# A two-block kernel on one core: new keys stage, expert stage with 4 KB rows and outputs put off by a block, output weights split early

## The reference, cut to what matters

```python
# merge and output of each mixer: mixed (512 x 1024) @ w_out (1024 x 1024), then x = layer_norm(ALPHA * x + ...)
# experts: 32, top 4 of them for each token, in blocks of up to 128 tokens of one expert
hb = xb @ w_exp_in[e] + b_exp_in[e]            # 128 x 1024 @ 1024 x 2048
g = jnp.minimum(hb[:, :D_FF], SWIGLU_LIMIT)
u = jnp.clip(hb[:, D_FF:], -SWIGLU_LIMIT, SWIGLU_LIMIT)
a = g * jax.nn.sigmoid(SWIGLU_ALPHA * g) * (u + 1.0)
y = a @ w_exp_out[e] + b_exp_out[e]            # 128 x 1024 @ 1024 x 1024
# compressed keys and values: 31 blocks of 32 positions, 16 apart, of each of 2 groups of width 64
blocks = src.reshape(B, S, G, dk)[:, blk_idx] + cmp_pos[None, None, :, None, :]
blocks = blocks.transpose(0, 3, 1, 2, 4).reshape(B, G, n_cmp, CMP_BLOCK * dk)
return jax.nn.gelu(blocks @ w1) @ w2           # w1: 2048 x 128, w2: 128 x 64
```

## Time and profile before

| | us |
|---|---|
| median of 3 runs (2675.25 to 2684.84) | 2681.73 |
| the profiled execution's own time | 2683.39 |
| its span | 2681.4 |
| PE busy | 2223.4 (83%) |
| DVE busy | 1728.8 (64%) |
| ACT busy | 1336.6 (50%) |
| POOL busy | 383.9 (14%) |
| expert stage, first to last product | 645.4 to 1880.6 |

### The profile page before, as it was taken

The page is one execution under the profiler, slowest core; times in us unless marked ns, Lnnn a source line. Parts: engine busy times, 40 slices in busy tenths (PEclk is TensorE's granted clock), DMA queues, the critical chain, the costliest instruction groups (busy, mean ns, idle before and its releaser), DMA issues. The chain is left out here.

```text
span 2681.4 us, 31345 instructions
## 1 busy us (share of the span) xinstructions
PE 2223.4 (83%) x10176; PEld 1775.4 (66%) x10176; DVE 1728.8 (64%) x2113; ACT 1336.6 (50%) x1452; POOL 383.9 (14%) x224
## 2 busy tenths in 40 slices
PE   4969879855999999999999999999158988885586
PEld 3747668654777777777777777777058666674564
DVE  4463511347899889989898989898620454457634
ACT  2333433225777777777777777776010343341130
POOL 0101134302111111111111111111000000000032
PEclk9989999966999999999999999999575677997888
DMA  5122033126999999999999999997470001010030
GB/s 185 32 102 55 16 95 94 63 67 244 343 350 365 351 349 354 361 350 347 357 362 349 347 357 362 349 348 274 162 141 16 9 0 47 24 47 0 19 107 32
DMA packets 305951, 524.83 MB, mean 196 GB/s; under 512 B 24055, under 2 KB 87551, under 8 KB 304525
## 3 DMA queue, kind: packets, MB, share of 16 engines
q1 hardware_dynamic: 287020, 486.59, 51.7%
q0 software_dynamic: 9504, 34.61, 3.3%
q10 hardware_dynamic: 9376, 2.98, 0.7%
HBM read 503.12 MB, written 26.78 MB: 198 GB/s over the span
## 5 line engine op out<-in xcount | busy, mean ns | idle before, releaser
L1370 DVE TENSOR_TENSOR piece_lower<-piece,moe_upper 128x2048 fp32r<-128x2048 f32 x384 | 870.2, 2287 | 120.7 <-ACT moe_upper L1302 120.7
L1302 ACT CAST moe_upper<-piece 128x2048 fp32r<-128x2048 f32 x384 | 727.5, 1911 | 112.2 <-PE bank L1242 103.9
L1240 PE MATMUL bank<-moe_upper,x_hi 128*128 128x512 f32 x1536 | 643.2, 419 | 0.0
L1242 PE MATMUL bank<-moe_upper,x_hi 128*128 128x512 f32 x1536 | 606.7, 395 | 0.0
L1241 PE MATMUL bank<-piece_lower,x_hi 128*128 128x512 f32 x1536 | 606.7, 395 | 0.0
L1242 PEld LDWEIGHTS bank<-moe_upper,x_hi 128*128 128x128 f32 x1536 | 289.8, 189 | 67.1
L1241 PEld LDWEIGHTS bank<-piece_lower,x_hi 128*128 128x128 f32 x1536 | 290.6, 189 | 62.1
L1240 PEld LDWEIGHTS bank<-moe_upper,x_hi 128*128 128x128 f32 x1536 | 291.6, 190 | 60.0
L1201 POOL COPY moe_dst<-row 128x1 uint32 x32 | 46.2, 1443 | 829.6 <-ACT moe_y L1289 829.6
L264 PE MATMUL bank<-const,xs 128*128 128x128 f32 x96 | 20.7, 386 | 96.7 <-DVE xs L235 96.7
L1293 ACT CAST x_hi<-bank 128x512 fp32r<-128x512 f32 x64 | 37.0, 578 | 108.9 <-PE bank L1248 108.9
(11 more groups left out here) (479 smaller groups left out, 4017.7 us busy)
## 6 DMA issues: line engine op xcount, KB each, us to landing
piece<-in_w_exp_in_dram SPq DMA_DIRECT2D x256, 1024.0 KB, 6.3
piece<-in_w_exp_out_dram SPq DMA_DIRECT2D x128, 1024.0 KB, 5.9
combine_ys<-y_slots SPq DMA_DIRECT2D x8, 1024.0 KB, 9.3
ahead<-in_w_in_dram SPq DMA_DIRECT2D x3, 2048.0 KB, 8.2
ahead<-in_w_in_dram SPq DMA_DIRECT2D x4, 1536.0 KB, 6.6
diff_raw<-in_w_in_dram SPq DMA_DIRECT2D x8, 512.0 KB, 5.1
band_raw<-in_w_in_dram SPq DMA_DIRECT2D x8, 512.0 KB, 5.1
ahead<-in_w_in_dram SPq DMA_DIRECT2D x8, 512.0 KB, 4.7
```

Of the source, the lines that this page charges most:

```text
L1240: nc.tensor.matmul(bank, hi[:, t, :], upper[u][:, t, :], start=False, stop=False)
L1242: done = nc.tensor.matmul(bank, lo[:, t, :], upper[u][:, t, :], start=False, stop=last and t == 3)
L1302: nc.scalar.copy(upper[h % SPLIT][:, :, :], ring[s][:, :, :]).then_inc(hi_ready, 1)
L1370: nc.vector.tensor_tensor(lower[s][:, :, :], ring[s][:, :, :], upper[h % SPLIT][:, :, :].bitcast(F32), ALU.subtract).then_inc(lo_ready, 1)
```

## The change

- **Experts.** A piece is now 128 partitions x 2 rows x 1024 columns (rows of 4 KB), 8 pieces into g and u, 4 into the output; one piece feeds two banks. The output product of block j-1 is put off into the iteration of block j, behind that block's input product: PE does 8 input pieces of block j, transposes the halves of block j-1's activations after pieces 3 and 4, waits for their lower parts, transposes the next tokens, then does the 4 output pieces of block j-1. The first iteration has 8 pieces, and a `last` part after the loop does the last output. Two iterations stand ahead of the loop, and one `If` guards a pair. The block count is rounded up to an even one, and every expert gets at least one block. `sg`, `g` and `u` are handled on DVE and ACT one iteration later.
- **Route.** SP issues the first 8 loads (expert 0) at once, behind the biases'. DVE has four more small operations and three more drains.
- **Output weights.** The first half of `w_out` is split in the stage before, on ACT and DVE (`output_upper`, `output_lower`); the second half's lower part moves from POOL to DVE, 3 tiles behind each row block.
- **Keys stage.** All loads move to SP at the stage's start. The two halves of a block's 32 positions now stand on the two halves of the partitions, so that a matmul sums over 128 rows and takes both groups' 62 columns: 16 matmuls for keys and 16 for values. ACT copies the projections to both halves of the partitions, shifted by 16.

The diff, cut to its core; where a part stands nested, eight spaces of indentation are left out:

```diff
+    for f in (NK - 2, NK - 1):
+        act.wait_ge(merged, f + 1)
+        gate(f, 0)
+        if f == NK - 1:
+            output_upper(nc, act, k)
+        gate(f, 1)
...
+    output_lower(nc, dve, k)
+    merge(NK - 1)
...
+def output_upper(nc, act, k):
+    act.wait_ge(k.ahead_in, k.ahead_loads)
+    for t in range(NK):
+        nc.scalar.copy(k.w_upper[:, t, :], k.ahead[:, t, :]).then_inc(k.output["w0_hi"], 1)
+def output_lower(nc, dve, k):
+    for t in range(NK):
+        dve.wait_ge(k.output["w0_hi"], NK * k.output.done["w0_in"] + t + 1)
+        split_lower(nc.vector, k.ahead[:, t, :], k.w_upper[:, t, :], k.ahead_lower[:, t, :])
...
-    for c in range(2):
-        act.wait_ge(*loaded[c])
-        for t in range(NK):
-            if c == 0:
-                nc.scalar.copy(m.hi[:, t, :], m_t[:, t, :]).then_inc(m_hi, 1)
-            nc.scalar.copy(w[c].hi[:, t, :], raws[c][:, t, :]).then_inc(w_hi, 1)
-@block.gpsimd
-def _(pool):
-    for c in range(2):
-        for t in range(NK):
-            pool.wait_ge(w_hi, 2 * NK * o + NK * c + t + 1)
-            split_lower(nc.gpsimd, raws[c][:, t, :], w[c].hi[:, t, :], w[c].lo[:, t, :]).then_inc(w_lo, 1)
+    for t in range(NK):
+        nc.scalar.copy(m.hi[:, t, :], m_t[:, t, :]).then_inc(m_hi, 1)
+    act.wait_ge(w1_in, 16 * o + 16)
+    for t in range(NK):
+        nc.scalar.copy(w[1].hi[:, t, :], raw1[:, t, :]).then_inc(w_hi, 1)
 @block.tensor
 def _(pe):
...
-                if i == 0:
-                    pe.wait_ge(w_lo, 2 * NK * o + NK * c + t + 1)
+                if n == NT:
+                    pe.wait_ge(w_lo, NK * o + t + 1)
...
+            for t in range(3 * n, min(3 * n + 3, NK)):
+                dve.wait_ge(w_hi, NK * o + t + 1)
+                split_lower(nc.vector, raw1[:, t, :], w[1].hi[:, t, :], w[1].lo[:, t, :]).then_inc(w_lo, 1)
...
-    col, kh = PIECES[h]
-    w = A["w_exp_in" if h < 8 else "w_exp_out"][0].rearrange("e (k p) n -> e p k n", p=P)
-    return w[ds(e, 1), :, 4 * kh:4 * kh + 4, col:col + 512].rearrange("o p k n -> (o p) k n")
+    col, pair = ((h // 4) * FF, h % 4) if h < INNER else (0, h - INNER)
+    w = A["w_exp_in" if h < INNER else "w_exp_out"][0].rearrange("e (k p) n -> e p k n", p=P)
+    return w[ds(e, 1), :, 2 * pair:2 * pair + 2, col:col + FF].rearrange("o p k n -> (o p) k n")
...
-    sp.wait_ge(expert_ready, 1)
-    e = sp.value_load(r.expert_i[0:1, 0:1], min_val=0, max_val=NE - 1)
-    for h in range(LOADED):
-        sp.dma_start(r.ring[h][:, :, :], weight_piece(A, e, h)).then_inc(r.piece_in[h], 16)
+    for h in range(INNER):
+        sp.dma_start(r.ring[h][:, :, :], weight_piece(A, 0, h)).then_inc(r.piece_in[h], 16)
...
-    nc.vector.tensor_scalar(nb[:, :], counts[:, :], 0.0, None, ALU.is_gt)
+    nc.vector.tensor_scalar(nb[:, :], counts[:, :], 0.0, None, ALU.is_ge)
...
+    nc.vector.tensor_scalar(r.expert[:, :], r.expert[:, :], float(NE - 1), None, ALU.min)
+    nc.vector.tensor_copy(total[:, 0:1], ends[:, NE - 1:NE])
+    dve.drain()
     nc.vector.tensor_copy(r.expert_i[:, 0:MAX_BLOCKS], r.expert[:, :])
-    nc.vector.tensor_copy(r.expert_i[:, MAX_BLOCKS:MAX_BLOCKS + 1], ends[:, NE - 1:NE])
-    dve.drain().then_inc(expert_ready, 1)
+    nc.vector.tensor_scalar(total[:, 1:2], total[:, 0:1], 1, None, ALU.bitwise_and)
+    dve.drain()
+    nc.vector.tensor_tensor(total[:, 0:1], total[:, 0:1], total[:, 1:2], ALU.add)
+    dve.drain()
+    nc.vector.tensor_scalar(r.expert_i[:, MAX_BLOCKS:MAX_BLOCKS + 1], total[:, 0:1], 2, None, ALU.subtract)
     for i in range(NT):
         nc.vector.tensor_tensor(dest[:, i, :], k.bank[i][:, 0:NE], starts[:, :], ALU.add)
...
+def each_pair(eng, iteration, last, before=None):
+    rest = eng.value_load(r.expert_i[0:1, MAX_BLOCKS:MAX_BLOCKS + 1], min_val=NE - 2, max_val=MAX_BLOCKS - 2)
     if before:
         before()
-    with eng.Fori(0, MAX_BLOCKS // 2) as q:
-        for p in range(2):
-            with eng.If(q * 2 + p < count):
-                body(q, p, q * 2 + p)
+    iteration(None, 0)
+    iteration(None, 1)
+    with eng.Fori(0, MAX_BLOCKS // 2 - 1) as q:
+        with eng.If(q * 2 < rest):
+            iteration(q, 0)
+            iteration(q, 1)
+    last(rest)
...
+    def iteration(q, p):
+        if is_first(q, p):
+            return
+        e = expert(at(q, p, 1))
+        for h in range(INNER):
+            load(e, slot(q, p, h), piece(q, p, h - LOADED), h)
+        e = expert(at(q, p, 1, -1))
+        for h in range(INNER, PIECES):
+            load(e, slot(q, p, h), piece(q, p, h - LOADED), h)
...
+        for t in range(2):
+            f = 2 * pair + t
+            for c in range(2):
+                to, cols = k.bank[bank + c][:, :], slice(512 * c, 512 * c + 512)
+                nc.tensor.matmul(to, hi[:, f, :], upper[u][:, t, cols], start=False, stop=False)
+                nc.tensor.matmul(to, hi[:, f, :], lower[s][:, t, cols], start=False, stop=False)
+                done = nc.tensor.matmul(to, lo[:, f, :], upper[u][:, t, cols], start=False, stop=f == NK - 1)
         done.then_inc(used, 1)
...
+    def iteration(q, p):
+        first = is_first(q, p)
+        pe.wait_ge(sel_ready, at(q, p, 1, 1))
+        pe.wait_ge(x_lo_ready, at(q, p, 2, 2))
+        for h in range(INNER):
+            if h % 4 == 0:
+                if not first:
+                    pe.wait_ge((g_ready, u_ready)[h // 4], at(q, p, 2))
+                for c in range(2):
+                    add_bias(p, h // 2 + c, FF * (h // 4) + 512 * c)
+            products(piece(q, p, h), slot(q, p, h), h, 2 * (h // 4), x_hi, x_lo)
+            if not first and h in (3, 4):
+                transpose_half(h - 3, at(q, p, 2, h - 4))
+        if not first:
+            pe.wait_ge(a_lo_ready, at(q, p, 2))
+        transpose_rows(1 - p, 16 * (p + 1) if q is None else q * 16 + 16 * (p + 2))
+        if not first:
+            if not is_second(q, p):
+                pe.wait_ge(y_sb, at(q, p, 2, -2))
+            outputs(1 - p, piece(q, p, INNER), [slot(q, p, h) for h in range(INNER, PIECES)])
+    def last(rest):
+        pe.wait_ge(x_lo_ready, rest * 2 + 6)
+        for half in range(2):
+            transpose_half(half, rest * 2 + 3 + half)
+        pe.wait_ge(y_sb, rest * 2 + 2)
+        pe.wait_ge(a_lo_ready, rest * 2 + 4)
+        outputs(1, rest * PIECES + LAST, [slot(0, 0, n) for n in range(4)])
...
+    def iteration(q, p):
+        first = is_first(q, p)
+        for h in range(INNER if first else PIECES):
+            upper_part(slot(q, p, h), h, landed(q, p, h), piece(q, p, h - SPLIT + 1))
+            if h == 3 and not first and not is_second(q, p):
+                output(piece(q, p, 0), at(q, p, 1, -1))
+            if not first and h in (7, 8):
+                activations_hi(h - 7, at(q, p, 2, h - 8))
+            if not first and h in (9, 10):
+                gate_sigmoid(h - 9, at(q, p, 2, h - 8))
+        if first:
+            for half in range(2):
+                gate_sigmoid(half, half + 1)
+        tokens_hi(at(q, p, 2, 3))
...
+    each_pair(act, iteration, last, lambda: tokens_hi(1))
...
+    def iteration(q, p):
+        first = is_first(q, p)
+        if not first:
+            inputs(INNER if is_second(q, p) else piece(q, p, -4))
+        for h in range(INNER if first else PIECES):
+            if h == INNER:
+                gates(piece(q, p, 4))
+            lower_part(piece(q, p, h), slot(q, p, h), h)
+            if h == 0:
+                select(at(q, p, 1), p)
+            if not first:
+                if h in (0, 2):
+                    gated_input(h // 2)
+                if h in (1, 3):
+                    activations(h // 2, at(q, p, 2, h // 2 - 1))
+                if h in (8, 9):
+                    activations_lo(h - 8, at(q, p, 2, h - 9))
+        if first:
+            gates(4)
+        tokens_lo(at(q, p, 2, 3))
+    def last(rest):
+        inputs(rest * PIECES + LAST - 4)
+        for half in range(2):
+            lower_part(rest * PIECES + LAST + half, slot(0, 0, half), half)
+            gated_input(half)
+            activations(half, rest * 2 + 3 + half)
+        for half in range(2):
+            activations_lo(half, rest * 2 + 3 + half)
+            lower_part(rest * PIECES + LAST + 2 + half, slot(0, 0, 2 + half), 2 + half)
...
+    with nc.allow_non_contiguous_dma(reason="positions by feature"):
+        for a in range(2):
+            sp.dma_start(pos[HD * a:HD * a + HD, :],
+                         A["cmp_pos_2"][0][16 * a:16 * a + 16, :].rearrange("l d -> d l")).then_inc(pos_in, 16)
+    for c, name in enumerate(("w_ck1_2", "w_cv1_2")):
+        w_halves = A[name][0].rearrange("(a l d) h -> a d l h", a=2, d=HD)
+        for a in range(2):
+            sp.dma_start(w1[c][HD * a:HD * a + HD, :, :], w_halves[a]).then_inc(c1_in[c], 16)
+    for c, name in enumerate(("w_ck2_2", "w_cv2_2")):
+        sp.dma_start(wc2[c][:, :], A[name][0]).then_inc(c1_in[0], 16)
...
-    sp.wait_ge(projected, p0 + 3)
-    for g in range(2):
```

(19 more changed lines are left out.)

315 lines of the change are left out of this document (138 added, 177 removed).

## The result

| | before | changed |
|---|---|---|
| median us | 2683.28 (2675.25 to 2686.35, 4 runs) | 2557.21 (2556.54 to 2558.8, 4 runs) |
| ratio | 1 | 0.9535, 95% interval 0.9513 to 0.9557 |
| span of the profiled execution | 2681.4 | 2554.7 |

The time fell by 126.1 us; 121.1 was forecast. To see where it went, the start of one instruction at each stage's edge is read from both traces. The third column is the kernel before in a second execution, run later ("before_again").

The account below looks back on a forecast made before the run. PE was taken to bound the expert stage, waiting 1.94 us per block for DVE; -48.5 + 3.3 - 61.9 - 14.0 = -121.1 us gave a median of 2560.6 us, range 2543 to 2606 with rivals, own range 2545 to 2578.

Parts of the forecast that it names:

- A, the block: Expert stage: PE's 1.94 us of waits per block go, 38.65 to 36.7 us; 32 blocks save 62.1 us.
- the new wait ahead of the output pieces: Expert stage: PE waits for the activations' lower part; the chain takes 5.2 us beside 5.6 us of PE work.
- The slack of 0.4 us: Expert stage: what is left between PE's 5.6 us for pieces 6 and 7 and ACT's and DVE's 5.2 us.
- A, fill and drain: Ends of the expert loop: PE waits 5.7 us after the first iteration and 7.9 us more after its last input piece.
- The DMA side: Expert stage: a block moves 13.63 MB, which at 36.7 us needs 371 GB/s; the transfers were expected to keep up.
- 385 GB/s: Expert stage: rate taken for rows of 4 KB, the middle between 364 and 405 GB/s at a full share of queues.
- rival 1: Expert stage: transfers bind at 364 GB/s, 37.4 us per block, +24 us, 2585 us; sign a share of 0.99 or more; chance 0.18.
- B: Start of the experts: route's small DVE operations cost 1.0 us, the first product comes 2.3 us later; sum +3.3 us.
- C: Keys stage: ACT's first cast 23.3 us earlier, compression to its result 11.4 us against 50.0, -38.6; sum -61.9 us.
- D: Output stages: with weights split ahead PE waits only for m; 7.0 us saved in each of two stages, -14.0 us.
- the bounds of 8.2 (none) and 5.9 (four tiles): Output stages: gain per stage, 8.2 us at the upper clock level throughout, 5.9 us with four tiles at half level.

Follow-up runs that it names:

- transpose_5_6: Changed kernel, but PE transposes the halves of the activations after pieces 5 and 6 in place of 3 and 4; 2693.78 us, ratio 1.005.
- turns_16: Kernel before with 16 turns of the expert loop in place of 24, nothing else changed; 2676.34 us, ratio 0.9981.
- rows_2k: Changed kernel, but each 1 MB piece is loaded by two transfers of 512 columns, rows of 2 KB as before; 2557.71 us.
- experts_only: Kernel before with the changed route and expert stages alone; 2643.25 us, ratio 0.9842.
- start_fill: Changed kernel with ACT and DVE doing the first two weight pieces ahead of the tokens, in the first and second iterations; 2545.64 us, ratio 0.9495.
- outputs_only: Kernel before with the changed merge, silu and output stages alone; 2677.32 us, ratio 0.9975.

## Why the prediction was right

Faster by 126 us against 121. The mechanisms of the four groups hold, and the total is within 5 us in part by luck: several terms were off and cancelled.

- **A, the block.** Right in mechanism and size: the pauses for `moe_a` and for the activations' lower part went, the new wait ahead of the output pieces costs nothing, the period is 36.53 (36.7 said). The slack of 0.4 us is 0.54 in the trace, and the similar chain of transpose_5_6 gives 2.69 of wait where its working has 3.0. The block saved 38.54 - 36.53 = 2.01 us and not 1.94, 64.3 us for 32 in place of 62.1.
- **A, fill and drain.** The mechanism was right, the pauses too large: 5.15 and 5.75 against 5.7 and 7.9. For the skipped turns I took 0.42 each; PE's 2.14 for 8 is 0.27. But the half level behind the pauses, which I had at nothing, costs some 1.7 and 3.3 (estimates from the windows), so the two ends cost 15.9 and not 13.6. With the block, -64.3 + 15.9 = -48.4: that the stage came out at the -48.5 of the forecast is two errors of some 2 us that cancel.
- **A, what I left out.** I read the 6.77 us in which ACT skips unused turns and counted the new ones, but never asked which engine skips the old ones last. It was POOL, behind the last scatter, and the barrier waited for it: 5.5 us, shown by turns_16.
- **The DMA side.** The choice of 385 GB/s was harmless, its reason wrong. A share of 0.97 was not the queues' limit: rows_2k shows 1.03 and 374 GB/s with rows of 2 KB, and the share of 0.99 that I would have read as rival 1's sign stands in the changed kernel with PE never waiting.
- **B.** +4.0 in all against +3.3: 0.8 in route (I said 1.0; experts_only has it too), 3.2 at the first product (2.3).
- **C.** The issue on ACT was worth 23.9 (23.3 said). The compression came to 7.25 us and not 10.7, since I priced its passes between two rates of the kernel before. The slower was at half level. The quicker, 0.96 / 7 = 0.137, was a misreading: 0.96 us is the duration of a row with the modelled end of its last matmul, and from start to start a pass took 0.113 at the upper level. The new ones ran at 1.00 throughout; that they would was not forecast, and why the clock fell 2.6 us (before) to 5.4 us (experts_only) behind the old compression's start but not in the 7.25 us of the new one isn't shown. Against the 87.2 of the four other traces the gain is 40.5 and not 43.5.
- **D.** -6.8 and -5.7 against -7.0 twice, in mechanism and size as worked out. In the first stage PE does 8 matmuls at half level, 2.7 tiles, which by the bounds of 8.2 (none) and 5.9 (four tiles) gives 6.7; in the second it does 12, four tiles, which gives 5.9.
- **Not foreseen: +5.0** in the attention stage. The 5.5 of POOL and the 4.9 more of the keys stage (1.9 against the 87.2) were gains that I had not counted, and these 5.0 take half or more of them back, which is why the sum looks better than its parts. That is luck.

What stays open is what settles the clock's course in the attention stage. Its length was 166.1 to 183.2 us over all traces, in the order of its time at half level, and 176.0 in four of them (the changed kernel twice, rows_2k, start_fill). It doesn't simply follow from the stage's start time: 2068.9 gave 182.9 (outputs_only) and 2070.2 gave 176.4 (turns_16). No run changed it by itself, and all but two kernels have a single trace.
